# A last feed-forward whose units run as 512-column products over a high and a low operand, with one eviction for two tiles

## The chip, the cores and the metric

The kernel runs on one core of one Trainium2 chip. Its time is the device time of one launch, in microseconds. Three runs of the kernel before gave 2199.34, 2200.89 and 2201.28 us, so the median is 2200.89 us.

## The reference, cut to what matters

The program is two stacks of transformer blocks on 256 latent tokens of 1024 features. The second stack has two layers and carries 256 context tokens too. The change touches only the feed-forward of the very last layer, which works on the 256 latent tokens alone:

```python
# second_block, last layer (i = 1), latent tokens only
x = _layer_norm(alpha * x + g1 * y, ln1_g[i], ln1_b[i])
x = _layer_norm(alpha * x + g2 * _mlp(x * (1 + sc2) + sh2, mlp_w1[i], mlp_w2[i]), ln2_g[i], ln2_b[i])
# _mlp(a, w1, w2): hidden = relu(a @ w1) ** 2, 4096 wide; out = hidden @ w2
```

Products are in float32 quality. A number is held as a high part (rounded to the type that TensorE takes, `fp32r`) and a low part (the rest), and a product is high*high + high*low + low*high.

## The kernel before, in words

**Units.** Weights come in units of 128 x 2048 float32 (16 tiles of 128 x 128, 1 MB), by two DMA transfers of half a unit each, into a ring of three slots (`SLOTS = 3`). The transfer of unit u+3 is issued on the SP queue when TensorE has finished unit u. ScalarE rounds each half to `w_hi` (L1467), VectorE computes `w_lo = w_raw - w_hi` (L2156). Both do so two units ahead (`ahead(u)` splits unit u+2 in the turn of unit u). TensorE waits for `lo_split` of a half before it first uses that half.

**The last feed-forward** (`run_mlp(1)`) has 32 units: 4 up, 4 down, 4 up, 4 down, and so on, four quarters of each. I number them 0 to 31: up units are 0 to 3, 8 to 11, 16 to 19, 24 to 27; down units are 4 to 7, 12 to 15, 20 to 23, 28 to 31. An up quarter makes 8 tiles of the hidden layer (two per unit), and the down quarter behind it uses these 8 tiles in each of its four units. Units 0 to 3 (`plain_up`) work on an input that is normalized afterwards and are not part of the change, nor are the down units 4 to 7 and 28 to 31.

**A unit on TensorE** (`fm_unit`, `fm_tile`): two products, one after the other, each over 8 tiles k. For each k there are three matmuls of 256 columns into one PSUM bank: `w_hi` with the high operand, `w_hi` with the low operand, `w_lo` with the high operand. So a unit has 48 matmuls. A product goes to a bank of ring A (banks 0, 1) or ring D (banks 2, 3), and waits until the product two before in its ring is evicted. In unit 8, the first with freshly normalized operands, the two products are interleaved k by k, and each k waits for `operand`. In the first unit of a down quarter (12, 20, 28) tile k waits for `hid_ready`.

**Evictions of an up unit**, one tile at a time: ScalarE takes max(x, 0) from PSUM (L1491), VectorE squares (L3146), rounds to the high part (L3148), and computes the low part (L2156 with `hid_both`), which raises `hid_ready`. Behind the second tile come the two `w_lo` halves of unit u+2. **Of a down unit**: VectorE adds each tile to the sum `y_acc` (in `qk`, L3222), then splits, and in units 12 to 15 and 20 to 23 computes one tile of the modulation of another layer part (`ada_tile`, L2191, two passes of 128 x 1024). ScalarE has no eviction there and casts weights as they land. In units 16 to 19 VectorE also rescales two tiles of X (L2260), in 24 to 27 it adds two tiles of the sum to X (L3243).

**Fresh operands.** During down units 4 to 7 VectorE normalizes two tiles of X per unit, ScalarE modulates them (L2064) and rounds (L1498), VectorE makes the low part (L2156 with `a_both`). The last two tiles, 6 and 7, are made behind the `w_lo` halves of the turn of unit 7.

**The four wide stages** of the first stack (`run_ffn`) already use 512-column matmuls: `wide_high` multiplies `w_hi` with the high and low operand side by side into a whole bank of 512 columns, `wide_lows` adds `w_lo` times the high operand into the second half of the bank, and the eviction adds the two halves (ScalarE copy L1892, VectorE add L2936). Their up part takes the same 16 wide and 16 narrow matmuls per unit as the changed units do.

The order of the work is written out by hand; there is no scheduler.

Of the kernel before, what the change touches and what calls it, by code (L numbers as in the profile page):

```python
# [117 lines left out]

def last_ring(quarter, j):
    return "AD"[j % 2] if quarter < 3 else None  # L120
FIRST_SMALL = slice(0, SMALL["ones"].stop)
# [26 lines left out]
def program(nc, weights, small, x_t, c_rows, ctx_t, na_bias, na_bv, out_t):  # L148
    with ExitStack() as ctx:
# [147 lines left out]


        def pair_banks(j):
            return [(0, 1), (2, 3)][j % 2]  # L300
# [169 lines left out]
        plain_hi, plain_lo = (h[:, 6 * S:6 * S + KD * PLAIN].rearrange("p (k t) -> p k t", k=KD) for h in (hid_hi, hid_lo))  # L470
        last_hi, last_lo = ([h[:, c:c + S] for c in [S * k for k in range(6)] + [20 * S, 21 * S]] for h in (hid_hi, hid_lo))
        mean_row = p_ring[:, 2, LAT]
        plain_out = [p_ring[:, j, LAT] for j in range(2)]
# [59 lines left out]
        def _(pe):  # L533
# [823 lines left out]
            def run_mlp(i):  # L1357
# [6 lines left out]
                def hidden(c):  # L1364
                    return [(hi[k][:, c], lo[k][:, c]) for k in range(KD)]

                def plain_up():
                    plain = [(plain_hi[:, k, :], plain_lo[:, k, :]) for k in range(KD)]

                    def arrives(k):  # L1370
                        pe.wait_ge(plain_ready, k + 1)
                        if k == 5:
                            n["ln"] += 1
                            n["chain"] += 1
                            layer_totals(slice(0, S), TOK, KD)
                            layer_mean(slice(0, S), MEAN)

                    def spreads(k):
                        if k == 2:
                            layer_spread(0, S // P, SPREAD, 0)  # L1380

                    fm_unit(PLAIN_RINGS[0], plain, arrives, True)
                    fm_unit(PLAIN_RINGS[1], plain, spreads, True)
                    for rings in PLAIN_RINGS[2:]:
                        fm_unit(rings, plain)

                def up(many=4, quarter=3):
                    for j in range(many):
                        fm_unit(2 * (last_ring(quarter, j) or "A"), a)

                def down(q, many=4, between=None):
                    for j in range(many):
                        early = i == 1 and q == 0 and j == 0
                        fm_unit(2 * (last_ring(q if i == 1 else 3, j) or "D"), hidden(slice(0, T)),
                                None if j else lambda k: wait(pe, hid_ready, hid0 + KD * q + k + 1), early, between if j == 1 else None)

# [5 lines left out]
                for q in range(3):  # L1402
                    down(q)
                    if i == 1 and q == 0:
                        operands()
                    up(quarter=q + 1 if i == 1 else 3)
                down(3, 4 if i else 2, lambda: shift_mean(T))
# [46 lines left out]
        def _(act):  # L1454
# [572 lines left out]
            def run_mlp(i):  # L2027
# [15 lines left out]
                def plain_up(j):  # L2043
                    u, _ = next_unit(PLAIN_RINGS[j])
                    ahead(u)
                    for m in range(2):
# [10 lines left out]
                        nc.scalar.copy(last_hi[k], y).then_inc(hid_h, 1)  # L2057

                def modulated(k):
                    n["norm"] += 1  # L2060
# [6 lines left out]
                for q in range(4):  # L2067
                    for j in range(4):
                        if i == 0 and q == 0:
                            up("DAEA"[j], j > 0)  # L2070
                        elif q == 0:
                            plain_up(j)
                        else:
                            up(last_ring(q if i == 1 else 3, j) or "A")
                    if i == 1 and q == 0:
                        for j in range(5):
                            for k in (2 * j - 2, 2 * j - 1) if j else []:
                                modulated(k)
                            if j < 4:
                                skip(2 * last_ring(q, j))  # L2080
                    elif q < 3:
                        for j in range(4):
                            skip(2 * (last_ring(q if i == 1 else 3, j) or "D"))
                if i == 0:
                    stream_layer()
                else:
                    layer_units(cols, T, i)

# [53 lines left out]
        def _(dve):  # L2142
# [986 lines left out]
            def run_mlp(i):  # L3129
# [8 lines left out]
                def up(q, ring="A", split_ahead=True):  # L3138
# [55 lines left out]
                for at in range(3):  # L3194
                    for q in range(4):
                        if i == 0 and at == 0:
                            up(q, "DAEA"[q], q > 0)
                        elif at == 0:
                            plain_up(q)
                        else:  # L3200
                            up(q, last_ring(at if i == 1 else 3, q) or "A")
                        if i == 1 and at == 2:
# [4 lines left out]
                    for q in range(4):  # L3207
                        ring = last_ring(at if i == 1 else 3, q) or "D"
                        u, made = next_unit(2 * ring)
# [24 lines left out]
                if i == 1:  # L3234
                    dve.wait_ge(ada_sum, 2 * MOD_TILES + 4)
                    finish_mods(MOD_LAST, MOD_TILES)
                    sync()
                for q in range(4):
                    up(q)
                    for k in (2 * q, 2 * q + 1):  # L3240
# [12 lines left out]
                else:  # L3253
                    layer_units((1, 5), cols, T)

# [219 lines left out]
```

## Time and profile before

| | |
|---|---|
| median of 3 runs | 2200.89 us |
| the profiled execution | 2199.01 us |
| its span in the trace | 2197.2 us |
| TensorE matmul busy | 2170.6 us, 99% |
| VectorE busy | 1782.4 us, 81% |
| ScalarE busy | 1171.2 us, 53% |
| mean granted TensorE clock | 0.998 of 2.4 GHz |

The profiled execution took 1.81 us more than its span, which is what lies around the traced part. "Busy" of TensorE is a union of modelled intervals that overlap, so 99% says that it never waits for long, not that each matmul runs at its shortest. The work behind the last matmul (the final normalization and the store of the output) takes the rest of the span.

### The profile page before, as it was taken

To read this page: it belongs to the slowest core of one execution; us is meant where nothing else is said; L and a number is where in the kernel's file an instruction comes from. 1 tells how busy PE (TensorE), PEld (TensorE's weight loads), DVE (VectorE), ACT (ScalarE), POOL (GpSimd) and SP (SyncE) were. 2 spreads that over 40 slices of the span, in tenths; PEclk is the share of its full clock that TensorE was granted. 3 is DMA by queue.
4 is the path that set the end of the run, shared out by engine and by line. 5 is a ranking of instruction groups with operands and counts; after the bars stand their busy time and mean duration, and the time that the engine had idled before them with its cause. 6 is when DMAs were issued, how large, how long until landed. Compare 5 with 4: busy or idle time off the path is not lost.

```text
span 2197.2 us, 38028 instructions
## 1 busy us (share of the span) xinstructions
PE 2170.6 (99%) x15136; PEld 1946.0 (89%) x15136; DVE 1782.4 (81%) x3522; ACT 1171.2 (53%) x2051; POOL 0.2 (0%) x4
## 2 busy tenths in 40 slices
PE   9999999999999999999999999999999999999998
PEld 8888889898899988996988987898888889979998
DVE  8879978689887898888898777578877876478898
ACT  5776556565554655558655646452222236376533
POOL 0000000000000000000000000000000000000000
PEclk9999999999999999999999999999999999999999
DMA  8326665467665676770676531015454523435663
GB/s 274 121 90 234 220 211 198 161 214 235 195 219 175 208 241 201 220 221 22 228 238 201 176 125 58 20 62 179 158 186 167 167 79 106 135 98 167 208 237 119
DMA packets 115377, 372.04 MB, mean 169 GB/s; under 512 B 12416, under 2 KB 22272, under 8 KB 115200
## 3 DMA queue, kind: packets, MB, share of 16 engines
q1 hardware_dynamic: 106688, 359.97, 50.0%
q10 hardware_dynamic: 8512, 9.63, 1.4%
q8 instruction: 120, 1.97, 0.4%
q14 instruction: 57, 0.47, 0.1%
HBM read 367.46 MB, written 1.05 MB: 168 GB/s over the span
## 4 chain that ended last, share of the span: by engine, by line
PE 92%; DVE 6%; ACT 2%; issue 1%; ACTq 0%; DVEq 0%
PE ps L538 88%; DVE hid_f L2551 1%; PE ps L882 1%; DVE hid_f L2573 1%; PE ps L818 1%; PE ps L866 1%; DVE w_lo L2156 1%; PE ps L988 0%; ACT p_ring L1607 0%; DVE X L2288 0%; PE ps L806 0%; DVE a_both L2156 0%; DVE X L2435 0%; DVE recip L2567 0%; ACT hid_f L1674 0%
## 5 line engine op out<-in xcount | busy, mean ns | idle before, releaser
L538 PE MATMUL ps<-a_both,w_hi 128*128 128x256 f32 (+1 forms) x4816 | 1028.4, 328 | 1.3 <-DVE a_both L2156 0.7
L538 PEld LDWEIGHTS ps<-a_both,w_hi 128*128 128x128 f32 x4816 | 806.3, 190 | 77.8 <-DVE a_both L2156 3.3
L2156 DVE TENSOR_TENSOR w_lo<-w_raw,w_hi 128x1024 fp32r<-128x1024 f32 (+3 forms) x630 | 703.9, 1144 | 75.1 <-ACT w_hi L1467 59.4
L538 PE MATMUL ps<-a_both,w_lo 128*128 128x256 f32 (+1 forms) x3112 | 693.7, 292 | 0.0
L1467 ACT CAST w_hi<-w_raw 128x1024 fp32r<-128x1024 f32 (+3 forms) x428 | 404.0, 973 | 272.6 <-DMA w_raw<-weights 270.9
L538 PEld LDWEIGHTS ps<-a_both,w_lo 128*128 128x128 f32 x3112 | 506.4, 191 | 17.2
L538 PE MATMUL ps<-hid_both,w_hi 128*128 128x512 f32 (+2 forms) x2184 | 512.9, 347 | 1.0 <-DVE hid_both L2348 0.5
L538 PEld LDWEIGHTS ps<-hid_both,w_hi 128*128 128x128 f32 x2184 | 377.5, 189 | 54.5 <-issue 5.4
L538 PE MATMUL ps<-hid_both,w_lo 128*128 128x256 f32 (+2 forms) x1444 | 330.0, 304 | 0.0
L538 PEld LDWEIGHTS ps<-hid_both,w_lo 128*128 128x128 f32 x1444 | 229.9, 191 | 14.0
L1475 ACT CAST w_hi<-w_raw 128x1024 fp32r<-128x1024 f32 (+1 forms) x198 | 202.3, 1022 | 0.2 <-DMA w_raw<-weights 0.2
L1892 ACT COPY p_ring<-ps 128x512 f32<-128x512 f32 x88 | 51.7, 587 | 135.5 <-PE ps L538 117.7
L2191 DVE CUSTOM_DVE_ANT_1 ps<-pe_sb,X 128x1024 f32<-128x1024 f32 x96 | 118.0, 1229 | 1.6
L1491 ACT ACTIVATE p_ring<-ps 128x512 f32<-128x512 f32 (+1 forms) x56 | 28.2, 506 | 169.1 <-PE ps L538 168.8
L2191 DVE CUSTOM_DVE_ANT_0 ps<-pe_sb,c_late 128x1024 f32<-128x1024 f32 x88 | 108.2, 1230 | 3.2
L1674 ACT ACTIVATE hid_f<-hid_f,negmax 128x128 f32<-128x128 f32 (+1 forms) x192 | 94.1, 498 | 14.1 <-DVE negmax L2551 13.6
L538 PE MATMUL ps<-w_hi,a_both 128*128 128x256 f32 (+1 forms) x448 | 93.3, 304 | 0.0
L2936 DVE TENSOR_TENSOR p_ring<-ps,p_ring 128x512 f32<-128x512 f32 x88 | 60.6, 688 | 38.6 <-ACT p_ring L1892 38.6
L538 PEld LDWEIGHTS ps<-w_hi,a_both 128*128 128x128 f32 x448 | 72.1, 191 | 4.2 <-issue 1.4
L2156 DVE TENSOR_TENSOR hid_both<-t_ring,hid_both 128x256 fp32r<-128x256 f32 (+1 forms) x152 | 72.2, 477 | 3.2 <-ACT hid_both L2057 1.3
L1895 ACT ACTIVATE p_ring<-p_ring 128x256 f32<-128x256 f32 x88 | 36.8, 419 | 58.6 <-DVE p_ring L2938 58.6
L538 PE MATMUL ps<-w_lo,a_both 128*128 128x256 f32 (+1 forms) x224 | 67.4, 301 | 0.0
(261 smaller groups left out, 1934.2 us busy)
## 6 DMA issues: line engine op xcount, KB each, us to landing
w_raw<-weights SPq DMA_DIRECT2D x496, 512.0 KB, 4.5
pe_sb<-weights SPq DMA_DIRECT2D x96, 512.0 KB, 5.4
w_raw<-weights SPq DMA_DIRECT2D x64, 384.0 KB, 3.3
w_raw<-weights SPq DMA_DIRECT2D x64, 320.0 KB, 3.7
pe_sb<-na_bias ACTq DMA_DIRECT2D x32, 128.0 KB, 2.2
X<-x_t SPq DMA_DIRECT2D x2, 512.0 KB, 6.7
X<-c_rows ACTq DMA_DIRECT2D x2, 512.0 KB, 7.6
qk<-qk ACTq DMA_DIRECT2D x4, 256.0 KB, 6.4
```

The lines of the kernel that those rows point to most:

```text
L538: return nc.tensor.matmul(out, stationary, moving, start=start, stop=stop)
L818: last = nc.tensor.matmul(ps[:, o, q], v, t_ring[:, e, t], start=j == 0, stop=j == len(it["pv"]) - 1, skip_group_check=True)
L866: last = nc.tensor.transpose(ps[:, banks[r], at // 2:at // 2 + HD], p_pair(name, b)[half(r), at:at + P], ident[half(r), half(r)])
L1467: nc.scalar.copy(high, whole).then_inc(hi_split, 1)
L1475: nc.scalar.copy(w_hi[:, u % SLOTS, c], raw(u, c)).then_inc(hi_split, 1)
L1491: nc.scalar.activation(dst, src, func or ACT.Copy, **kw).then_inc(taken[ring], 1)
L1674: last = nc.scalar.activation(at, at, ACT.Exp, bias=negmax[:, i % 4, x:x + 1], scale=-1.0, accum_out=sums[:, i % 4, x:x + 1])
L1892: nc.scalar.copy(low_slot, ps[:, at, S:2 * S]).then_inc(low_copied, 1)
L1895: nc.scalar.activation(gate_sum, gate_sum, ACT.Silu).then_inc(silu_done, 1)
L2156: return v.tensor_tensor(out, a, b.bitcast(F32), ALU.subtract)
L2191: v.tensor_tensor_reduce(to, ada_w[:, a % 2, :].rearrange("p (a b) -> p a b", b=S), c, 1.0, 0.0, ALU.mult, ALU.add, mod[:, a, s_:s_ + 1]). ...
L2936: v.tensor_tensor(both, ps[:, made[0][0]:made[1][0] + 1, 0:S], low_slot, ALU.add).then_inc(taken["A"], 1)
```

## The change

The 12 up units 8 to 11, 16 to 19 and 24 to 27 and the 8 down units 12 to 15 and 20 to 23 are issued by a new function `wide_unit`: the 512-column products of both tiles first, then the 256-column `w_lo` products of both. It waits at its start until both banks of its ring are free. ScalarE copies the second halves of both banks in one instruction (`low_halves`), VectorE adds them to the first halves in one instruction of 512 columns (`both_halves`), and all that follows is 512 columns wide for the two tiles of a unit together: the squared relu in one instruction on VectorE, the high part on ScalarE, the low part on VectorE. One `w_lo` half of unit u+2 now stands between the square and the low part, on VectorE and likewise on ScalarE. All these units alternate between ring A and ring D (before, quarter 3 did not), and unit 28 moves to ring A.

On TensorE:

```diff
+                def wide_unit(ring, xs, arrives=None):
+                    u, made = start_unit(2 * ring)
+                    for _, p, _ in made:
+                        start_product(ring, p)
+                    lower = bank_pair(made).start
+                    for at, (bank, _, _) in enumerate(made):
+                        for k, x in enumerate(xs):
+                            if arrives and at == 0:
+                                arrives(k)
+                            wide_high(ps[:, bank, :], u % SLOTS, (bank - lower) * KD + k, x, k == 0, False)
+                    for bank, _, (ready, _) in made:
+                        wide_lows(ps[:, bank, :], u % SLOTS, (bank - lower) * KD, xs, True).then_inc(ready, 1)
...
-                def up(many=4, quarter=3):
+                def up(many=4):
                     for j in range(many):
-                        fm_unit(2 * (last_ring(quarter, j) or "A"), a)
+                        if i == 1:
+                            wide_unit(last_ring(j), wide_parts(LAT), operand_at)
+                        else:
+                            fm_unit("AA", a)
...
+                        if i == 1 and q in (1, 2):
+                            wide_unit(last_ring(j), last_both, None if j else arrives)
+                            continue
+                        ring = last_ring(j) if i == 1 and q == 0 else "A" if i == 1 and j == 0 else "D"
+                        fm_unit(2 * ring, hidden(slice(0, T)), None if j else arrives, early, between if j == 1 else None)
```

On ScalarE:

```diff
+                def low_halves(ring):
+                    u, made = next_unit(2 * ring)
+                    for _, _, (s_, count) in made:
+                        wait(act, s_, count)
+                    if lows:
+                        before, p = lows[-1]
+                        act.wait_ge(taken[before], p + 1)
+                    lows.append((ring, made[1][1]))
+                    nc.scalar.copy(low_slot, ps[:, bank_pair(made), S:2 * S]).then_inc(low_copied, 1)
+                    return u
+                def wide_up(j):
+                    u = low_halves(last_ring(j))
+                    split_half(u + 2, 0)
+                    r = cnt.next("relu")
+                    cnt.next("relu")
+                    act.wait_ge(hid_f, r + 2)
+                    nc.scalar.copy(last_pairs[j][0], t_ring[:, j % 2, :]).then_inc(hid_h, 2)
+                    split_half(u + 2, 1)
...
+                    elif i == 1 and q < 3:
+                        for j in range(4):
+                            ahead(low_halves(last_ring(j)))
```

On VectorE:

```diff
+                def both_halves(made, ring, j):
+                    both = gate_up_slot[j % 2]
+                    for m in made:
+                        ready(m)
+                    n["low_part"] += 1
+                    dve.wait_ge(low_copied, n["low_part"])
+                    v.tensor_tensor(both, ps[:, bank_pair(made), 0:S], low_slot, ALU.add).then_inc(taken[ring], 2)
+                    dve.wait_ge(taken[ring], made[1][1] + 1)
+                    return both
+                def wide_up(j):
+                    ring = last_ring(j)
+                    u, made = next_unit(2 * ring)
+                    both, y = both_halves(made, ring, j), t_ring[:, j % 2, :].rearrange("p (a t) -> p a t", a=2)
+                    r, h = cnt.next("relu"), cnt.next("hid")
+                    cnt.next("relu")
+                    cnt.next("hid")
+                    dve.wait_ge(hid_ready, h)
+                    v.scalar_tensor_tensor(y, both, 0.0, both, ALU.max, ALU.mult).then_inc(hid_f, 2)
+                    split_half(u + 2, 0)
+                    dve.wait_ge(hid_h, h + 2)
+                    minus(last_pairs[j][1], t_ring[:, j % 2, :], last_pairs[j][0]).then_inc(hid_ready, 2)
+                    split_half(u + 2, 1)
+                    ada_tiles()
+                def wide_down(j):
+                    ring = last_ring(j)
+                    u, made = next_unit(2 * ring)
+                    both, y = both_halves(made, ring, j), y_acc[:, 2 * j:2 * j + 2, 0:S]
+                    step(v.tensor_tensor(y, y, both, ALU.add))
+                    ahead(u)
+                    ada_tiles()
```

TensorE, the start of down unit 12, before (`hid_both` holds the hidden tiles; `taken_A` says that ring A is evicted):

```order
L538 MATMUL ps<-hid_both,w_hi 128x256 [waits hid_ready,taken_A,lo_split]
L538 MATMUL ps<-hid_both,w_hi 128x256
L538 MATMUL ps<-hid_both,w_lo 128x256
L538 MATMUL ps<-hid_both,w_hi 128x256 [waits hid_ready]
L538 MATMUL ps<-hid_both,w_hi 128x256
L538 MATMUL ps<-hid_both,w_lo 128x256
```

The same place and the unit behind it (13, ring D) after the change:

```order
L546 MATMUL ps<-hid_both,w_hi 128x512 [waits taken_A,hid_ready,lo_split]
L546 MATMUL ps<-hid_both,w_hi 128x512 [waits hid_ready] x7
L546 MATMUL ps<-hid_both,w_hi 128x512 [waits lo_split]
L546 MATMUL ps<-hid_both,w_hi 128x512 x7
L546 MATMUL ps<-hid_both,w_lo 128x256 x16
L546 MATMUL ps<-hid_both,w_hi 128x512 [waits taken_D,lo_split]
L546 MATMUL ps<-hid_both,w_hi 128x512 x15
L546 MATMUL ps<-hid_both,w_lo 128x256 x16
```

The eight tiles are now reached one matmul apart, where they were three apart. A unit on ring A waits for the second half of its weights before its ninth matmul. A unit on ring D has no such wait later on, because its first product falls on the upper bank (the count of products in ring D is odd there) and so uses the second half first: it waits for both halves at its start.

VectorE, the turn of up unit 11, before (`t_ring` is the square, `hid_both` the hidden tile):

```order
L3146 TENSOR_TENSOR t_ring<-p_ring 128x256 [waits taken_D,hid_ready]
L3148 CAST hid_both<-t_ring 128x256 [waits hid_f]
L2156 TENSOR_TENSOR hid_both<-t_ring,hid_both 128x256 [waits hid_h]
L3146 TENSOR_TENSOR t_ring<-p_ring 128x256 [waits taken_D]
L3148 CAST hid_both<-t_ring 128x256 [waits hid_f]
L2156 TENSOR_TENSOR hid_both<-t_ring,hid_both 128x256 [waits hid_h]
L2156 TENSOR_TENSOR w_lo<-w_raw,w_hi 128x1024 [waits hi_split] x2
```

and after, with the turn of down unit 12 behind it up to its `w_lo` halves:

```order
L3222 TENSOR_TENSOR p_ring<-ps,p_ring 128x512 [waits unit_done,low_copied,mid_ready]
L3234 SCALAR_TENSOR_TENSOR t_ring<-p_ring 128x512 [waits hid_ready,taken_D]
L2215 TENSOR_TENSOR w_lo<-w_raw,w_hi 128x1024 [waits hi_split]
L2215 TENSOR_TENSOR hid_both<-t_ring,hid_both 128x512 [waits hid_h]
L2215 TENSOR_TENSOR w_lo<-w_raw,w_hi 128x1024 [waits hi_split]
L3222 TENSOR_TENSOR p_ring<-ps,p_ring 128x512 [waits unit_done,low_copied,mid_ready]
L3245 TENSOR_TENSOR qk<-qk,p_ring 128x2x256 [waits taken_A]
L2215 TENSOR_TENSOR w_lo<-w_raw,w_hi 128x1024 [waits hi_split] x2
```

The low part of the two hidden tiles now stands behind one `w_lo` half, and the eviction begins only when the whole unit is done.

## Rows read from the trace of the kernel before

**Rows 1.** The page, section 1: busy time, share of the span, instructions.
```profile
PE 2170.6 (99%) x15136; PEld 1946.0 (89%) x15136; DVE 1782.4 (81%) x3522; ACT 1171.2 (53%) x2051; POOL 0.2 (0%) x4
```
**Rows 2.** Busy time by stretch, last feed-forward: stretch, length, busy of each engine, clock, DMA.
```profile
2100.00:2150.00 50.00, 50.00 (x419) 50.00 (x418) 45.98 (x79) 19.90 (x26) 0.00 (x0) 1.00 0.67 230
```
**Rows 3.** Chain that ended last, in order of time: start, us, what.
```profile
2001.89 183.06 PE ps L538 x1522
```
**Rows 4.** TensorE in order of time at unit 8: start us, us, instruction.
```profile
2046.12 0.40 PE L538 MATMUL ps<-a_both,w_hi 128*128 128x256 f32 x2
2046.48 0.40 PE L538 MATMUL ps<-a_both,w_hi 128*128 128x256 f32 x2
```
**Rows 5.** The same view in a wide stage: sixteen 512-column products.
```profile
619.68 3.79 PE L538 MATMUL ps<-hid_both,w_hi 128*128 128x512 f32 x16
```
**Rows 6.** ScalarE in order of time, wide stage, copies three units apart.
```profile
222.85 0.59 ACT L1892 COPY p_ring<-ps 128x512 f32<-128x512 f32 x1 [1.89 <-PE ps L538]
...
239.55 0.59 ACT L1892 COPY p_ring<-ps 128x512 f32<-128x512 f32 x1 [0.94 <-PE ps L538]
```
**Rows 7.** ScalarE, evictions of units 10 and 11 of the last feed-forward.
```profile
2063.66 0.38 ACT L1491 ACTIVATE p_ring<-ps 128x256 f32<-128x256 f32 x1 [2.50 <-PE ps L538]
...
2069.42 0.38 ACT L1491 ACTIVATE p_ring<-ps 128x256 f32<-128x256 f32 x1 [2.50 <-PE ps L538]
```
**Rows 8.** VectorE in order of time, the last hidden tile of unit 11.
```profile
2069.84 0.42 DVE L3146 TENSOR_TENSOR t_ring<-p_ring 128x256 f32<-128x256 f32 x1 [1.16 <-ACT p_ring L1491]
...
2070.62 0.42 DVE L2156 TENSOR_TENSOR hid_both<-t_ring,hid_both 128x256 fp32r<-128x256 f32 x1
```
**Rows 9.** VectorE, the turn of unit 7: weights, then operand tiles 6 and 7.
```profile
2047.39 2.35 DVE L2156 TENSOR_TENSOR w_lo<-w_raw,w_hi 128x1024 fp32r<-128x1024 f32 x2
2049.65 0.75 DVE L2156 TENSOR_TENSOR a_both<-p_ring,a_both 128x256 fp32r<-128x256 f32 x2
```
**Rows 10.** VectorE in a wide stage: the add that follows a copy of rows 6's kind.
```profile
240.17 0.69 DVE L2936 TENSOR_TENSOR p_ring<-ps,p_ring 128x512 f32<-128x512 f32 x1 [0.48 <-ACT p_ring L1892]
```
**Rows 11.** Groups of instructions by form: busy us, mean ns of one, idle before.
```profile
L2156 DVE TENSOR_TENSOR hid_both<-t_ring,hid_both 128x512 fp32r<-128x512 f32 x32 | 22.2, 693 | 1.1
L3148 DVE CAST hid_both<-t_ring 128x512 fp32r<-128x512 f32 x32 | 13.7, 427 | 1.1
L2156 DVE TENSOR_TENSOR w_lo<-w_raw,w_hi 128x1024 fp32r<-128x1024 f32 x494 | 590.2, 1219 | 64.3 <-ACT w_hi L1467 49.1 <-ACT w_hi L1475 15.0
L1467 ACT CAST w_hi<-w_raw 128x1024 fp32r<-128x1024 f32 x312 | 318.5, 1047 | 245.8 <-DMA w_raw<-weights 244.3 <-issue 0.8
L1997 ACT CAST a_both<-qk 128x512 fp32r<-128x512 f32 x8 | 5.0, 621 | 14.7 <-DVE qk L3077 14.7
```
**Rows 12.** VectorE, the turn of down unit 13 and the start of the next.
```profile
2081.22 2.35 DVE L2156 TENSOR_TENSOR w_lo<-w_raw,w_hi 128x1024 fp32r<-128x1024 f32 x2
2083.49 1.22 DVE L2191 CUSTOM_DVE_ANT_0 ps<-pe_sb,c_late 128x1024 f32<-128x1024 f32 x1
...
2085.96 0.42 DVE L3222 TENSOR_TENSOR qk<-ps,qk 128x256 f32<-128x256 f32 x1
2086.64 0.42 DVE L3222 TENSOR_TENSOR qk<-ps,qk 128x256 f32<-128x256 f32 x1 [0.27 <-PE ps L538]
```
**Rows 13.** VectorE, the X work in units 16 and 24.
```profile
2102.03 0.73 DVE L2260 TENSOR_SCALAR X<-X,alpha_g,alpha_b 128x256 f32<-128x256 f32 x2
...
2148.56 0.88 DVE L3243 SCALAR_TENSOR_TENSOR X<-qk,mod,X 128x256 f32<-128x256 f32 x2
```
**Rows 14.** SP queue and ScalarE: a unit's weights from issue to cast.
```profile
2075.11 0.81 SPq L514 DMA_DIRECT2D w_raw<-weights  x2
...
2080.27 1.05 ACT L1467 CAST w_hi<-w_raw 128x1024 fp32r<-128x1024 f32 x1 [0.21 <-DMA w_raw<-weights]
```
**Rows 15.** TensorE by stretch at the program's end: length, busy (x), clock, DMA.
```profile
2184.00:2186.00 2.00, 0.96 (x9) 1.00 0.00 0
...
2190.00:2192.00 2.00, 0.00 (x0) 0.50 0.02 4
```

More of the change, by code:

```diff
@@ L116, with last_ring @@
 PLAIN_RINGS = ["AA", "DD", "AA", "DD"]
-def last_ring(quarter, j):
-    return "AD"[j % 2] if quarter < 3 else None
+def last_ring(j):
+    return "AD"[j % 2]
 FIRST_SMALL = slice(0, SMALL["ones"].stop)
@@ L296, in unit, with bank_pair @@
             return u, made
+        def bank_pair(made):
+            lower = min(bank for bank, _, _ in made)
+            return slice(lower, lower + 2)
         def pair_banks(j):
@@ L471, in program @@
         last_hi, last_lo = ([h[:, c:c + S] for c in [S * k for k in range(6)] + [20 * S, 21 * S]] for h in (hid_hi, hid_lo))
+        last_both = [(hi, lo, hid_both[:, :, S * k:S * k + S])
+                     for hi, lo, k in zip(last_hi, last_lo, [*range(6), 20, 21])]
+        last_pairs = [[h[:, S * k:S * k + 2 * S] for h in (hid_hi, hid_lo)] for k in (0, 2, 4, 20)]
         mean_row = p_ring[:, 2, LAT]
@@ L1385, in plain_up, with arrives @@
                         fm_unit(rings, plain)
-                def up(many=4, quarter=3):
+                def up(many=4):
                     for j in range(many):
-                        fm_unit(2 * (last_ring(quarter, j) or "A"), a)
+                        if i == 1:
+                            wide_unit(last_ring(j), wide_parts(LAT), operand_at)
+                        else:
+                            fm_unit("AA", a)
                 def down(q, many=4, between=None):
+                    def arrives(k):
+                        wait(pe, hid_ready, hid0 + KD * q + k + 1)
                     for j in range(many):
                         early = i == 1 and q == 0 and j == 0
-                        fm_unit(2 * (last_ring(q if i == 1 else 3, j) or "D"), hidden(slice(0, T)),
-                                None if j else lambda k: wait(pe, hid_ready, hid0 + KD * q + k + 1), early, between if j == 1 else None)
+                        if i == 1 and q in (1, 2):
[3 more added lines that the diff above has]
+                        fm_unit(2 * ring, hidden(slice(0, T)), None if j else arrives, early, between if j == 1 else None)
                 if i == 0:
@@ L1405, in run_mlp @@
                         operands()
-                    up(quarter=q + 1 if i == 1 else 3)
+                    up()
                 down(3, 4 if i else 2, lambda: shift_mean(T))
@@ L2072, in run_mlp @@
                             plain_up(j)
+                        elif i == 1:
+                            wide_up(j)
                         else:
-                            up(last_ring(q if i == 1 else 3, j) or "A")
+                            up()
                     if i == 1 and q == 0:
@@ L2086, in run_mlp @@
                 else:
-                    layer_units(cols, T, i)
+                    layer_units(cols, T, i, first="A")
             def run_na(_):
@@ L3207, in run_mlp @@
                     for q in range(4):
-                        ring = last_ring(at if i == 1 else 3, q) or "D"
+                        if i == 1 and at > 0:
+                            wide_down(q)
+                            continue
+                        ring = last_ring(q) if i == 1 else "D"
                         u, made = next_unit(2 * ring)
@@ L3237, in run_mlp @@
                     sync()
+                sync()
                 for q in range(4):
-                    up(q)
+                    if i == 1:
+                        wide_up(q)
+                    else:
+                        up(q)
                     for k in (2 * q, 2 * q + 1):
@@ L3253, in run_mlp @@
                 else:
-                    layer_units((1, 5), cols, T)
+                    layer_units((1, 5), cols, T, first="A")
             def run_na(_):
```

10 lines of the change are left out of this document (6 added, 4 removed).

## The prediction

> **What bounds the kernel now.** I read the page's busy times first, then the table of stretches, then the chain, then the engines in order of time around the changed units. TensorE is busy for 99% of the span [rows 1], and for the whole of a stretch inside the last feed-forward at full clock, while VectorE is busy for 46 of its 50 us there [rows 2]. The chain of waits through this stage is one piece of matmuls, 183.06 us long [rows 3]. So two things count: how fast matmuls follow each other, and whether TensorE has to wait, which it does not do now. VectorE has some 8% to give, and that is a mean over quarters that differ.
>
> **What the wide form saves.** In unit 8 three matmuls of 256 columns start every 0.36 us (2046.12 and 2046.48 [rows 4]), 0.120 us each, so a unit is 48 x 0.120 = 5.76 us; the evictions of units 10 and 11 confirm it, 2069.42 - 2063.66 = 5.76 us [rows 7]. A 512-column matmul takes about 0.227 us: 16 of them stand in 3.79 us, of which the last one's tail, some 0.16 us, lies over the next [rows 5]. A pair of 256-column matmuls costs 0.240, so merging it saves 0.013 us, and 16 pairs save 0.21 us. The wide stage has units of just this mixture (16 wide, 16 narrow), and three of them take 239.55 - 222.85 = 16.70 us, 5.57 each [rows 6]. I take 5.57, as it is measured with all that goes with it: 0.19 us per unit, and **20 units save 3.8 us** (4.3 by the single matmuls, as the other end).
>
> The Trainium skill ("TensorE: Matmul & The Clock Gate", section "Back-to-back issue gap") gives N / 2.4 GHz plus about 2.5 ns between matmuls. This trace does not agree: 256 columns are 106.7 ns and take 120. By that rule the 320 merged pairs would save 320 x 2.5 ns = 0.8 us (an estimate from that page), and the total below would be 3 us later.
>
> **What the change lets become late.** The chunks of work behind a unit get fewer and longer, and they start later. I measure from E, the moment at which TensorE has issued the unit's last matmul; ScalarE starts the eviction 0.26 us later (the next unit of the row at 2069.42 starts at 2069.16 by the 5.76 grid from 2046.12 [rows 4, 7]).
>
> *Operands at unit 8.* VectorE makes operand tiles 6 and 7 behind the weights in the turn of unit 7, from 2049.65 on: two in 0.75 us, so done at 2050.07 and 2050.40 [rows 9]. Nothing in this part moves. Before, unit 8 went through both products k by k and came to tile 7 at 2046.12 + 7 x 0.72 = 2051.16, late enough. Now it comes to tile 7 after seven wide matmuls, at 2046.12 + 1.59 = 2047.71, and has to wait until 2050.40 plus some 0.05 us of signalling. **A wait of 2.75 us.** Queued behind it is the whole of TensorE's stream.
>
> *Hidden tiles at units 12, 20 and 28.* Before, the last hidden tile of unit 11 was ready at 2070.62 + 0.42 = 2071.04 [rows 8], 1.88 us after E = 2069.16, and wanted at 7 x 0.36 = 2.52 us: hidden. After the change both last tiles pass one chain: ScalarE's copy of 512 columns, start E + 0.26, 0.59 long [rows 6], to 0.85; VectorE's add, 0.04 later, 0.69 long [rows 10], to 1.58; the square of 512 columns, 0.03 later. The trace has no such form from SBUF; its nearest are 0.69 (a subtraction of two 512-column tiles) and 0.43 (a copy) [rows 11]. Having two tensor inputs it is nearer the first: 0.69, to 2.30. Then ScalarE rounds 512 columns, 0.62 [rows 11], to 2.96. VectorE meanwhile has begun a `w_lo` half at 2.22; two halves take 2.27 us [rows 12], so one holds it until 3.36; then the low part, 0.69, to 4.05, and 4.10 at TensorE. TensorE wants tile 6 after six wide matmuls, at 1.36. **A wait of 2.74 us at unit 12 and at unit 20.** Unit 28 keeps its three matmuls per tile and wants tile 6 at 6 x 0.36 = 2.16: **1.94 us.** Before, tile 6 had been evicted half a unit earlier. The ends: if the `w_lo` half did not stand between, 3.00 + 0.69 + 0.05 = 3.74, a wait of 2.4; if a late cast of weights on ScalarE (1.05 [rows 11]) pushed the rounding, up to 3.8.
>
> *VectorE in the down quarters.* Before, a down unit cost it two adds, two halves (2.27) and a modulation tile (2.47, from 2083.49 to 2085.96), and it then waited 0.27 us for the next tile [rows 12]. Now it has an add of 0.69 + 0.03, an add into the sum of 0.61 (512 columns without a wait behind it), 2.27 and 2.47: 6.07 us against 5.57 of TensorE. It falls back 0.50 us per unit, so it starts 1.5 us late on unit 15. Its second half for unit 17 is then ready at E + 4.58 + 1.5 + 0.05 = 6.13, and unit 17 is on ring D, wants both halves at its start at 5.57, and waits 0.56. In up units it has add 0.72, square 0.61, half 1.14, low part 0.61, half 1.14 = 4.2 us, plus 0.65 for X [rows 13] in quarter 2, and makes the second half ready at E + 5.19, only 0.38 before a ring D unit wants it. Being 0.75 late at unit 17, it lets unit 19 wait 0.43. In quarter 3 it starts 0.5 later still (it completes the modulation first) and X costs 0.8 [rows 13]: 0.56 at unit 25, and at unit 27, after 1.37 of lateness at unit 25, 1.05. **Together 2.6 us**; this is the least sure term, between nothing (if VectorE is 0.5 us quicker per unit than I count) and 5.
>
> *What costs nothing.* The weights' transfers: the second half is cast 5.2 us after the issue at a unit's end [rows 14], and the new order on ScalarE needs it 1.7 us after the next E, at 7.3. The banks: a ring is taken two units later and evicted 1.6 us after E. A wait may also cost a restart of TensorE, which no row shows; between nothing and 0.3 us for each of 8 waits (the first matmul then no longer lies over another). I take nothing.
>
> **The sum.** -3.8 + 2.75 + 2.74 + 2.74 + 1.94 + 2.6 = +8.9 us. The work behind the last matmul is the same. From the profiled execution, 2199.01, this gives 2207.9; the median of the runs is 1.9 us above it, so **2209.8 us**, 0.4% slower. A measurement of this kernel tells about 0.2% (4.4 us) from no change.
>
> **Rivals.**
> 1. *The late weights do not come about*, only the four waits for operands and hidden tiles: +6.3, **2207.2**. For it: VectorE's lateness rests on two instructions that the trace does not show in this form. Against it: the modulation tile alone takes 2.47 us. Chance 0.2.
> 2. *The wide form gains what it does in the wide stages and nothing waits*: -3.8, **2197.1**, not slower. Its place is the end of units 11, 19 and 27 and the operands of unit 8. It decides from the point at which the tiles are ready within 1.36 us (1.59) of the next unit's start, where I count 4.1 (4.3). For it: the same form runs in the wide stages with TensorE full. Against it: no stage there consumes a tile so soon after its eviction, and copy and two passes alone are 2 us. Chance 0.1, with all that ends within 0.2% or below.
> 3. *The clock falls in a wait.* At the end of the program TensorE is half idle from 2184 on and still has its full clock; it has the half level, 1.2 GHz, in the stretch from 2190 on, in which it does nothing [rows 15]. No wait in the body is as long as the 2.7 us above. Should the clock fall in each of the four and stay low for one unit of 5.57 us, these take twice as long: 4 x 5.57 = 22 us more, **2232**. Against it: 2.7 us of rest against 5 us of thin work and rest in the one case that the rows show. Chance 0.06.
>
> On 3 the Trainium skill (the same page, section "HAM oscillation — how this bites in real kernels") says that waits between bursts of matmuls bring the clock down again and again. By that rule the time would be the one of rival 3 if these waits are long enough; that the clock does fall without work, rows 15 agree.
>
> **How the numbers follow.** My forecast has 0.64, the rivals 0.2, 0.1 and 0.06. The lower ends of the waits (2.75 + 2 x 2.4 + 1.6 = 9.1) with the larger saving and no late weights give +4.9, 2205.8; the upper ends (restarts 2.4, late weights 5) give +13.7, 2214.6. I reach a little toward rival 2 below: **2203.5 to 2214.5**. Slower by over 0.2% means above 2205.3: 0.86. Within 0.2%: 0.10. Faster: 0.04.
>
> **What would show it.** In the changed trace TensorE should wait for `a_both` once, at unit 8, some 2.7 us; for `hid_both` three times, 2.7, 2.7 and 1.9; and a few times for `w_lo`, under 1.1 us each, at ring D units. Copies of ScalarE inside a quarter should be 5.57 us apart. The prediction is wrong if the units are closer together than that, if the waits on `hid_both` are under 2 us or absent, or if the clock column is below 1.00 in the stage.

## The result and the profile after

The changed kernel takes **2222.98 us** (median of 4 runs, 2215.9 to 2227.36), the kernel before 2201.09 in the same session (4 runs, 2199.34 to 2208.37): ratio 1.009, interval [1.0067, 1.0112]. It is slower, as forecast, but by 22 us and not by 9, and outside the range that I gave. The same kernel, run a second time later together with the kernel before, gave 2215.36 (7 runs, 2214.3 to 2218.45), ratio 1.0054 [1.0034, 1.0074]. I call such a group of runs a submission. That two submissions of one program differ by 7.6 us is half of the story.

First TensorE at unit 8 in the changed kernel, in order of time (start us, us, instruction, and in brackets the idle time before it and who ended it). It answers to [rows 4].

```profile
2061.65 1.55 PE L546 MATMUL ps<-a_both,w_hi 128*128 128x512 f32 x6
2065.68 2.68 PE L546 MATMUL ps<-a_both,w_hi 128*128 128x512 f32 x10 [2.49 <-DVE a_both L2215]
```

Two things stand here. There are six wide matmuls and then 2.49 us of idle time, the first wait of the forecast. And the unit begins at 2061.65, where it began at 2046.12 before [rows 4]: 15.5 us are already lost ahead of the first instruction that the change touches. The view of busy time by stretch (stretch, length, busy of TensorE, weight load, VectorE, ScalarE, POOL, granted clock, DMA share, GB/s) shows where, in the changed kernel:

```profile
75.00:80.00 5.00, 5.00 (x39) 4.31 (x39) 3.78 (x4) 3.19 (x5) 0.00 (x0) 0.82 0.50 167
80.00:85.00 5.00, 5.00 (x25) 5.00 (x25) 3.32 (x13) 4.86 (x7) 0.00 (x0) 0.50 0.45 184
...
995.00:1000.00 5.00, 5.00 (x26) 5.00 (x25) 0.00 (x0) 1.76 (x8) 0.00 (x0) 0.50 0.00 0
```

and the kernel before in a stretch of the same work, 45 matmuls at full clock where 25 stand above:

```profile
80.00:85.00 5.00, 5.00 (x45) 5.00 (x45) 3.91 (x17) 4.94 (x7) 0.00 (x0) 1.00 0.33 135
```

TensorE is full in both. Added up over windows of 1 us, its clock stands at the half level (1.2 GHz) for 13.7 us from 78 on and for 17.1 us from 989 on. Half of each is lost: 6.8 + 8.5 = 15.3 us.

The waits of the changed stage, grouped (who waits, for whom, then us in total, times, longest):

```profile
PE ps L546 <- DVE hid_both L2215: 7.3, 3, 2.7
PE ps L546 <- DVE w_lo L2215: 2.7, 4, 1.1
PE ps L546 <- DVE a_both L2215: 2.5, 1, 2.5
```

These are the ones that I named, in number and place, and in length to within 0.3 us. The clock behind the wait of unit 12, again TensorE in order of time and then by stretch:

```profile
2091.08 3.83 PE L546 MATMUL ps<-hid_both,w_hi 128*128 128x512 f32 x10 [2.68 <-DVE hid_both L2215]
2094.71 2.43 PE L546 MATMUL ps<-hid_both,w_lo 128*128 128x256 f32 x16
```

```profile
2090.00:2092.00 2.00, 0.92 (x4) 0.78 (x5) 2.00 (x3) 0.94 (x1) 0.00 (x0) 1.00 1.03 422
2092.00:2094.00 2.00, 2.00 (x7) 1.56 (x6) 0.20 (x1) 0.00 (x0) 0.00 (x0) 0.52 0.25 100
2094.00:2096.00 2.00, 2.00 (x11) 1.81 (x10) 0.00 (x0) 0.00 (x0) 0.00 (x0) 0.62 0.00 0
```

Ten wide matmuls stand in 3.83 us where ten behind unit 8's wait stand in 2.68. TensorE had waited 2.68 us and worked for about 1 us when the clock fell. From the start of unit 8 to the end the stage is 164.0 us long, 151.1 before: +12.9.

In the second submission's profile hardly anything is lost ahead (unit 8 starts at 2046.96; in the second profile of the kernel before it starts at 2046.77), but the clock falls behind all three waits for hidden tiles:

```profile
2078.00:2080.00 2.00, 2.00 (x6) 1.60 (x5) 0.00 (x0) 0.00 (x0) 0.00 (x0) 0.50 0.00 0
...
2130.00:2132.00 2.00, 2.00 (x12) 1.99 (x11) 0.00 (x0) 0.00 (x0) 0.00 (x0) 0.55 0.00 0
...
2180.00:2182.00 2.00, 2.00 (x11) 2.00 (x11) 0.50 (x2) 0.24 (x1) 0.00 (x0) 0.50 0.00 0
```

Each time 3.4 us at the half level, which cost 1.7. Its stage is 2213.6 - 2046.96 = 166.6 us.

### The profile page after: what moved, and what is told of

Its sections match the earlier page's. It is cut to its first block and busy times, and to the rows that moved or that the text cites. A ratio compares the mean times of both kernels' runs of the same rounds, so it can differ in the third digit from the quotient of the medians.

```text
span 2225.6 us, 37421 instructions
## 1 busy us (share of the span) xinstructions
PE 2187.0 (98%) x14816; PEld 1943.8 (87%) x14816; DVE 1785.9 (80%) x3486; ACT 1180.9 (53%) x2059; POOL 0.2 (0%) x4
## 5 line engine op out<-in xcount | busy, mean ns | idle before, releaser
L546 PE MATMUL ps<-a_both,w_hi 128*128 128x256 f32 (+1 forms) x4624 | 1005.6, 334 | 6.6 <-DVE a_both L2215 3.2
L546 PEld LDWEIGHTS ps<-a_both,w_hi 128*128 128x128 f32 x4624 | 781.1, 190 | 91.7 <-DVE a_both L2215 6.3
L546 PE MATMUL ps<-a_both,w_lo 128*128 128x256 f32 (+1 forms) x3112 | 664.0, 292 | 0.0
L546 PEld LDWEIGHTS ps<-a_both,w_lo 128*128 128x128 f32 x3112 | 493.9, 191 | 18.2
L1499 ACT CAST w_hi<-w_raw 128x1024 fp32r<-128x1024 f32 (+3 forms) x404 | 379.4, 970 | 244.7 <-DMA w_raw<-weights 243.2
L546 PE MATMUL ps<-hid_both,w_hi 128*128 128x512 f32 (+2 forms) x2056 | 499.4, 359 | 8.3 <-DVE hid_both L2215 7.3
L546 PEld LDWEIGHTS ps<-hid_both,w_hi 128*128 128x128 f32 x2056 | 361.5, 189 | 67.9 <-DVE hid_both L2215 9.1
L546 PE MATMUL ps<-hid_both,w_lo 128*128 128x256 f32 (+2 forms) x1444 | 310.7, 304 | 0.0
L1507 ACT CAST w_hi<-w_raw 128x1024 fp32r<-128x1024 f32 (+1 forms) x222 | 227.9, 1027 | 0.4 <-DMA w_raw<-weights 0.4
L1523 ACT ACTIVATE p_ring<-ps 128x512 f32<-128x512 f32 x32 | 19.0, 598 | 128.3 <-PE ps L546 128.0
```

Of the source, the lines that this page charges most:

```text
L546: return nc.tensor.matmul(out, stationary, moving, start=start, stop=stop)
L1499: nc.scalar.copy(high, whole).then_inc(hi_split, 1)
L1507: nc.scalar.copy(w_hi[:, u % SLOTS, c], raw(u, c)).then_inc(hi_split, 1)
L1523: nc.scalar.activation(dst, src, func or ACT.Copy, **kw).then_inc(taken[ring], 1)
```

## The experiments

Two theories for the part that the forecast missed. **A**: the clock falls because TensorE rests (in the three waits for hidden tiles), and the early falls are chance, which hits the kernel before as well. **B**: the change itself makes the clock fall, by its wide matmuls or by what it moves. The rows of clock below tell them apart. "Stage" is always from unit 8's first matmul to the end of the span.

**The kernel before, again.** No edit.

> The kernel before, unchanged. The changed kernel lost 15.5 us ahead of its changed part, in two stretches of identical code in which the granted clock was 0.50 (13 and 17 us long). Theory: such falls of the clock come at random in the two NSA stages, whatever the kernel; then of five more runs of this unchanged one some should show a mean clock below 0.997 and take 4 to 15 us more than 2200, and the profile's stage from unit 8 on (2046.1 to the end, 151.1 us) is as before. Rival: the change brings the falls about; then all runs lie within 2199 to 2202 with a mean clock of 0.998.

Measured: 2200.8 us (12 runs), ratio 0.9988 [0.997, 1.0006]. Nine runs at a mean clock of 0.998 take 2199.2 to 2201.2, three at 0.994 take 2208.0 to 2208.7. Beside the three submissions of experiments the kernel before ran 71 more times: 45 runs between 2199.2 and 2202.7, 23 between 2207.1 and 2208.7, 3 between 2213.9 and 2215.1. One stretch of 13.7 us at the half level costs 6.8, one of 17.1 costs 8.5: from the median of the lowest group, 2200.2, that gives 2207.0 to 2208.7, and two stretches give 2213.8 or more. The mean clocks of the three groups are 0.997 to 0.998, 0.994 to 0.995 and 0.991 to 0.992. So by time and mean clock an unchanged kernel has a long fall in 26 of 71 runs; where it lies no profile shows, as both profiles of the kernel before are of runs without one. Counted by time in the same way, with the first runs and these twelve, it is 30 of 87 for the kernel before and 30 of 90 for the changed kernel and its variants. That only the change brings it is refuted.

**The changed kernel, again.** No edit.

> The changed kernel, unchanged. Theory (random falls in identical code, waits in the changed part): a clean run takes 2210 us, others up to 15 us more, with the mean clock falling by 0.001 for every 4.4 us at half clock; from unit 8 on the profile shows about 163 us again. Rival (the change itself brings the early falls): every run is above 2214 with a mean clock of 0.996 or less.

Measured: 2215.36 us (7 runs), as told above: all seven at clocks of 0.995 to 0.997, none with an early fall. In the first submission three of four runs stood at 2221 to 2227 and clocks of 0.990 to 0.993, the fourth at 2215.9. So the median of the result carries about 7 us of chance, and 2215.4 is the changed kernel itself.

**Tiles 6 and 7 last** (`late`). Units 8, 12 and 20 take tiles 0 to 5 of both products and both operands first; unit 28 goes through its two products tile by tile (that is what `early` does).

```
+if arrives and (arrives is not operand_at or n["fresh"] is not None):
+    for part in (range(6), range(6, KD)):
+        for k in part:
+            arrives(k)
+            for bank, _, _ in made:
+                ...
+                mm(ps[:, bank, :], w_hi[...], xs[k][2], k == 0, False)
+        for bank, _, (ready, _) in made:
+            ...
+            last = wide_lows(ps[:, bank, :], ...)
+            ...
...
-early = i == 1 and q == 0 and j == 0
+early = i == 1 and q in (0, 3) and j == 0
```

> The changed kernel, but in units 8, 12 and 20 both products go through tiles 0 to 5 (wide and narrow) before either touches tiles 6 and 7, and unit 28 interleaves its two products. Tile 6 is then wanted 4.16 us after the unit's start (4.32 in unit 28) in place of 1.36 (2.16). Theory of the waits: the four waits of 2.5, 2.7, 2.7 and 1.9 us go, as does the fall of the clock behind the one at unit 12 (1.6 us): from unit 8 on 11 us less than the changed kernel, a clean run near 2199. Rival (the stage is slow through VectorE's load, and its time comes back as waits for weights): less than 5 us are won and the waits for w_lo grow to more than 6 us.

Measured: 2201.71 us (12 runs), ratio 0.9996 [0.9979, 1.0014]; the seven runs at 0.997 or 0.998 take 2199.4 to 2201.9, with a median of 2200.0. Its waits:

```profile
PE ps L546 <- DVE w_lo L2229: 2.6, 4, 1.1
```

All four operand waits are gone, and so is every fall of the clock in the stage, though its wide matmuls are as many as in the changed kernel. It is 15 us below the changed kernel's own 2215.4, where I had expected 11, with 9.7 us of idle time taken away: more went than the waits. B, in the form that the wide matmuls lower the clock, does not survive this.

**And the lower bank's product first** (`both`). As `late`, and wide units begin with the product whose `w_lo` half is ready first.

```
-for at, (bank, _, _) in enumerate(made):
+for at, (bank, _, _) in enumerate(sorted(made, key=lambda m: m[0])):
```

> As late, and in each wide unit the product of the lower bank comes first, so that units on ring D want the second half of their weights only 1.8 us after their start. Theory: the waits for w_lo (2.7 us in four places) go too, and what is left is the saving of the wide form: from unit 8 on about 147.5 us, 3.6 us less than the kernel before (151.1), a clean run at 2197. Rival (VectorE becomes the bound once nothing else waits): waits for w_lo of 2 us or more remain and the stage takes 150 us or more.

Measured: 2200.07 us (12 runs), ratio 0.999 [0.9972, 1.0008]; the eight runs at clock 0.998 have a median of 2199.1, the kernel before's runs at 0.998 or 0.997 in the same submission one of 2200.2. Its stage is 149.5 us, 2.0 more than I expected and just under the rival's 150: three waits for `w_lo` are left, 1.1 us in all, so a part of the rival is true. This is the best version, 1.1 us under the kernel before, and by its interval not to be told from it.

**The rests filled with work** (`fill`). This is the decisive experiment. The tiles come no earlier; TensorE repeats the unit's first matmul until they do, 10 or 11 times in the wide units and 15 times (`fill`) at unit 28.

```
+if arrives:
+    arrives(0)
+    for _ in range(10 if arrives is operand_at else 11):
+        if arrives is not operand_at or n["fresh"] is not None:
+            wide_high(ps[:, made[0][0], :], ..., xs[0], True, True)
...
+for _ in range(fill if j == 0 else 0):
+    tile_at(0)
+    mm(ps[:, bank, 0:T], w_hi[:, u % SLOTS, 0:P], xs[0][0], True, True)
```

> The changed kernel with idle time turned into work. TensorE repeats the first matmul of the unit, into the bank that the unit then starts anew, before it comes to the tiles it has to wait for: 10 times at unit 8, 11 times at units 12 and 20 (512 columns, 0.227 us each: 2.3 and 2.5 us), 15 times at unit 28 (256 columns, 0.120 each: 1.8 us). What it waits for is ready at the same time as before, so the path is as long and only the rest shrinks to 0.1 to 0.2 us. Theory A (the clock falls because TensorE rests; each of the three falls of some 3.4 us at the half level costs 1.7 us): clock 1.00 all through the stage, stage from the start of unit 8 to the end 166.6 - 5.1 = 161.5 us, undisturbed runs near 2209.5 to 2210. Theory B (the falls belong to the wide matmuls or to the load of this stage, and would come without the rests): falls in the stage as in the changed kernel, stage 166 to 167, 2214 to 2215. If both, A and a filler that costs something itself: 2211.

Measured: 2211.24 us (9 runs), ratio 1.0045 [1.0028, 1.0062]; seven runs at clock 0.998 take 2210.4 to 2211.7. The wait of unit 12, and the stretch around it:

```profile
2076.15 2.56 PE L546 MATMUL ps<-hid_both,w_hi 128*128 128x512 f32 x10 [0.19 <-DVE hid_both L2224]
```

```profile
2046.00:2100.00 54.00, 53.64 (x299) 46.31 (x298) 40.63 (x56) 25.33 (x33) 0.00 (x0) 1.00 0.61 202
2100.00:2150.00 50.00, 48.89 (x275) 42.38 (x274) 44.72 (x63) 22.37 (x28) 0.00 (x0) 1.00 0.65 220
2150.00:2196.00 46.00, 44.22 (x320) 41.59 (x319) 39.83 (x65) 19.14 (x28) 0.00 (x0) 1.00 0.36 120
```

The wide matmuls resume at the same moment as before (2076.15, in the changed kernel 2076.34), the rest is 0.19 us, and the clock stays at its full level throughout. The kernel does more work and is 4.8 us quicker (2215.4 against 2210.6, the median of these seven). Theory A is shown for the falls in the stage: take the rests away, by order as in `late` or by work as here, and these falls go. I had expected 2209.5 to 2210 and a stage of 161.5; the lowest runs take 2210.4, the stage 161.8. The two runs at 2219.0 and 2219.5, clock 0.994, have a long fall like those of the kernel before.

**Half of each rest filled** (`half`): 5, 6, 6 and 7 repeats in place of 10, 11, 11 and 15.

> As fill, with about half of each rest turned into work: 5, 6, 6 and 7 repeated matmuls, so rests of 1.3 us at units 8, 12 and 20 and 1.1 at unit 28. The path is again as long. If any rest of about a microsecond makes the clock fall: 2214 to 2215, with three or four falls in the stage. If the length of the rest decides, and only those of 1.9 us and more did it: no fall, 2209.5 to 2210.

Measured: 2212.45 us (9 runs), ratio 1.0056 [1.0036, 1.0075]; its lowest four take 2209.9 to 2211.2. In its profile the four rests are 1.29, 1.32, 1.32 and 1.07 us and the clock is 1.00 behind each:

```profile
2127.11 2.58 PE L546 MATMUL ps<-hid_both,w_hi 128*128 128x512 f32 x10 [1.32 <-DVE hid_both L2224]
```

```profile
2130.00:2134.00 4.00, 4.00 (x26) 3.55 (x25) 1.56 (x3) 2.31 (x3) 0.00 (x0) 1.00 0.33 86
```

Rests of 1.1 to 1.3 us are harmless there; two runs in the middle (2212.5 and 2212.9, clock 0.997) had a fall or two somewhere. The profile has one, at 2004, ahead of the stage.

**Only the down units narrow again** (`narrow_down`).

```
-if i == 1 and q in (1, 2):
+if i == 1 and q > 3:
...
-    ahead(low_halves(last_ring(j)))
+    skip(2 * last_ring(j))
...
-if i == 1 and at > 0:
+if i == 1 and at > 3:
```

> One part of the change alone: the 12 up units stay wide with both tiles evicted together, the 8 down units of quarters 1 and 2 are 256-column products again, each tile evicted by itself. By the terms of the forecast: the wide form gains 12 x 0.19 = 2.3; unit 8 waits 2.5; units 12, 20 and 28 all want hidden tile 6 at 2.16 us and get it at 4.10, so each waits 1.94 (5.8 in all); VectorE has its old work in the down units and falls back less, so 0 to 0.5 of late weights. Sum +6.0 to +6.5 against before, 2207 for undisturbed runs if no clock falls; with a fall of 1.7 us behind each of the three waits of 1.9 us, 2212. If the wide down units and not the up units were what costs, it would stand at 2202.

Measured: 2211.06 us (12 runs), ratio 1.0049 [1.0031, 1.0068]; three runs at clock 0.998 take 2208.2 to 2208.5. Its waits:

```profile
PE ps L546 <- DVE hid_both L2215: 6.0, 3, 2.2
PE ps L546 <- DVE a_both L2215: 2.5, 1, 2.5
```

So the joint eviction of the up units is what costs, and the waits for `w_lo` (none here) belong to the wide down units' load on VectorE, as forecast. 2207 was over 1 us too low for those three runs. In the profile, of a run at 0.997, the clock fell behind two of the three waits (2078 and 2173), between my two cases.

**Only the bank order** (`banks`): the one-line edit of `both`, by itself.

> The changed kernel with one edit: a wide unit computes the product of the lower bank first, whose low part of the weights is the half that is ready first. Units on ring D then need the second half of w_lo 5.6/2 us later. By the forecast's term the four waits for w_lo (0.6, 0.35, 0.6 and 1.1, together 2.6 us) go and nothing else moves: 2.6 us less than the changed kernel, undisturbed 2212 to 2212.8, waits for operands and hidden tiles as in the changed kernel. Rival: VectorE stays as late as it is, and what TensorE doesn't wait for there it waits for at units 20 and 28, whose hidden tiles come out of the same backlog: no gain, 2214 to 2215, with longer waits for hid_both.

Measured: 2217.8 us (6 runs), ratio 1.0067 [1.0046, 1.0088]; three runs carry an early fall, the other three take 2213.6 to 2214.6. Its waits:

```profile
PE ps L546 <- DVE hid_both L2215: 7.7, 3, 2.7
PE ps L546 <- DVE w_lo L2215: 0.6, 1, 0.6
```

Three of the four waits for `w_lo` are gone and the stage is 164.1 us, 2.5 less than the changed kernel's 166.6. The undisturbed runs lie 0.8 us or more above the 2212 to 2212.8 that I expected, and a little of the rival is true too: VectorE is as late as it was, and the wait at unit 28 grows from 1.92 to 2.34.

**The two halves of the repair** (`only8`, `only_hid`): `late` with unit 8 as in the changed kernel, and `late` with unit 8 alone mended.

```
-if arrives and (arrives is not operand_at or n["fresh"] is not None):
+if arrives and arrives is not operand_at:                        # only8
+if arrives is operand_at and n["fresh"] is not None:             # only_hid
```

> The changed kernel with the waits for hidden tiles taken away (units 12 and 20 consume tiles 6 and 7 of both operands last, unit 28 goes through both products tile by tile), the wait for operand tiles at unit 8 left. By the terms: as late, which stood 0.2 us below the kernel before, plus the wait of 2.4 us: undisturbed runs at 2202 to 2203. In four profiles the clock did not fall behind unit 8's wait, though it is as long as the others; if that is no accident, clock 1.00 in the stage here too and 2202.5; if it is chance, some runs show one fall of 3.4 us more and stand 1.7 higher, 2204.2.

Measured: 2204.2 us (12 runs), ratio 1.0017 [1.0, 1.0033]; the five lowest runs take 2202.6 to 2203.5, as expected, three more 2204.1 to 2205.6. The wait is there and nothing happens behind it:

```profile
2059.50 2.66 PE L546 MATMUL ps<-a_both,w_hi 128*128 128x512 f32 x10 [2.46 <-DVE a_both L2229]
```

> The other half: unit 8 consumes tiles 6 and 7 of both operands last and does not wait, the waits for hidden tiles at units 12, 20 and 28 stay (2.7, 2.7, 1.9). By the terms: the changed kernel's 2215.3 less 2.4, 2212.9 with three falls of 1.7 us, 2211.2 with two, 2207.8 with none. If the first wait had been what sets off the falls behind the later ones, there would be none and 2208.

Measured: 2212.64 us (7 runs), ratio 1.0051 [1.0032, 1.0071], six of them 2212.0 to 2214.8, with the clock down for 3.4 us behind each of the three waits (from 2076, 2127 and 2178). That is my case of three falls, 2212.9; the first wait does not set off the later falls.

## Why the prediction was wrong

The direction, the waits and their causes were right; the time was not. Taken by its own steps:

**The wide form's saving** was right. Copies of ScalarE inside a quarter, in the second profile of the changed kernel:

```profile
2099.17 0.59 ACT L2102 COPY p_ring<-ps 128x512 f32<-128x512 f32 x1 [3.09 <-PE ps L546]
2104.74 0.59 ACT L2102 COPY p_ring<-ps 128x512 f32<-128x512 f32 x1 [3.08 <-PE ps L546]
2111.13 0.59 ACT L2102 COPY p_ring<-ps 128x512 f32<-128x512 f32 x1 [0.52 <-issue]
```

5.57 us apart, as taken from the wide stage [rows 6]. `both`, which has hardly any waits, is 1.5 us shorter in the stage than before with 1.1 us of idle time left, so it gained at least 2.6, and 3.8 is nearer than the 0.8 that the other rule I weighed would give.

**The four waits** were right in their working (2.4 to 2.5, 2.68, 2.68 and 1.92 us of idle time; forecast 2.75, 2.74, 2.74 and 1.94). The chain behind unit 11 in the same profile, ScalarE's cast and VectorE around it:

```profile
2073.08 0.69 DVE L3222 TENSOR_TENSOR p_ring<-ps,p_ring 128x512 f32<-128x512 f32 x1 [1.22 <-ACT p_ring L2102]
2073.86 0.69 DVE L3234 SCALAR_TENSOR_TENSOR t_ring<-p_ring 128x512 f32<-128x512 f32 x1
2074.47 1.22 DVE L2215 TENSOR_TENSOR w_lo<-w_raw,w_hi 128x1024 fp32r<-128x1024 f32 x1
2075.60 0.69 DVE L2215 TENSOR_TENSOR hid_both<-t_ring,hid_both 128x512 fp32r<-128x512 f32 x1
```

```profile
2074.64 0.62 ACT L2111 CAST hid_both<-t_ring 128x512 fp32r<-128x512 f32 x1 [0.75 <-DVE t_ring L3234]
```

The square of 512 columns takes 0.69, of the two rows that I chose between [rows 11] the right one, and the low part stands behind one `w_lo` half.

**The restart, taken at nothing, is a term.** I gave it 0 to 0.3 us for each wait and took the lower end. The copies show it: from 2104.74 to 2111.13 is 6.39, or 0.82 more than a unit, where the wait shows 0.59 of idle time. In the rows a matmul that follows another starts some 0.2 us before that one's end [rows 4, 5], and behind a wait that is lost. In `fill`, whose clock is clean, unit 8 takes 2.83 more than a unit, units 12 and 20 2.97 and 2.99, the `w_lo` waits 0.83, 0.57, 0.85 and 1.34 (3.6 together, 2.6 forecast). With 2.1 at unit 28 (it starts at 2173.85 in the changed kernel, wants tile 6 at 2176.01 and resumes at 2178.10), -3.8 + 2.8 + 6.0 + 2.1 + 3.6 = **+10.7** in place of +8.9 (the forecast's terms as written add up to +9.0), and `fill`'s stage is 161.8 us against 151.1, which is 10.7.

**The step that failed is the clock.** The forecast's sum has no term for it, and rival 3, the fall behind waits, had a chance of 0.06, because the only rest with a fall that the trace showed was longer. It called the event unlikely and large, 5.57 us for each of four waits. The sign of being wrong that it named, a clock below 1.00 in the stage, is what the traces show. The fall is likely and small: in five profiles with those waits the clock fell behind 12 of 15 waits for hidden tiles, for 3.4 us each time, so 1.7 us a fall and up to 5.1 a run. 2200.2 + 10.7 + 5.1 = 2216.0 with all three, and the runs without an early fall lie at 2214.3 to 2218.45. With the early falls left out, the changed kernel is 2215.4, 5.6 above the forecast: 1.8 of restarts and 5.1 of clock, less 0.7 because the undisturbed kernel before stands at 2200.2 and not at 2200.9; 0.6 of that sum is not found again. Even so it lies outside the range, whose upper end had room for restarts and late weights and none for the clock.

**And the measurement's spread was taken too narrow.** I had three runs of the kernel before, all within 2 us, and concluded that 4.4 us can be told. It has a second place 7 to 8 us higher in a third of its runs. The median of four runs of the changed kernel fell into it.

On the Trainium skill's section on clock oscillation ("TensorE: Matmul & The Clock Gate", "HAM oscillation — how this bites in real kernels"), which I cited for rival 3: the runs agree that waits between pieces of matmuls bring the clock down again and again. The waits in the Trainium skill's case are of some 3 to 5 us; here rests of 1.9 to 2.7 us were enough, and those of 1.1 to 1.3 in `half` were not. The Trainium skill also has the clock stay up where the work between waits is long against them. The early falls do not fit that: they come with no wait, TensorE being busy for 5.00 of 5 us.

What stays open. Why unit 8's wait, 2.4 to 2.5 us long, has no fall behind it in any of five profiles (the changed kernel twice, `narrow_down`, `banks`, `only8`), where waits of 1.9 elsewhere have one. Why three of the 15 waits for hidden tiles have none: units 20 and 28 in the first profile of the changed kernel, unit 20 in `narrow_down`. And what starts the early falls; the profiles give only their place (below).

## What to carry to other kernels

Evicting two tiles together saves instructions but makes the last one late, so before it is done where the next unit consumes those tiles, compare the eviction's whole chain with the moment at which they are wanted; ordering the consumer so that the late tiles come last took back all 15 us here. Price a wait of TensorE as its idle time plus 0.2 to 0.4 us for the restart, plus 1.7 us for the clock behind waits like those of 1.9 and 2.7 us here, and if it can't be removed, fill it: repeating a matmul whose result is overwritten was worth 4.8 us. And look at the granted clock of every run before two medians are compared.

## What was not expected of the hardware

- The clock's falls come in fixed lengths. Added up over windows of 1 us, every stretch at the half level inside the program was 3.4, 13.7 or 17.1 us long, which is one, four and five times 3.4, in all twelve profiles; the program's end apart.
- The long ones come without a wait of TensorE, at the same place of the program: from about 983 in `late`, `banks` and `only8`, from 989 in the changed kernel (which was 6.8 us late by then), and once from 78, at the same step of the earlier layer. There 256-column products are followed by thin ones: 64 columns, then eight with only 64 rows of operand. TensorE in order of time in `late`:

```profile
982.92 0.28 PE L546 MATMUL ps<-w_lo,hid_both 128*128 128x64 f32 x1
983.13 1.35 PE L546 MATMUL ps<-qk 64*128 64x128 f32 x8
```

  "Busy" doesn't say that these products fill the engine as wide ones do: three of 64 columns take 0.34 us here, nearly as long as three of 256 columns, 0.36. The other profiles pass this place at full clock. A difference of code there was not tried, so that the thin products start the falls is not shown.
- A 3.4 us fall also came at about 2004 (2010 where an early fall had delayed it) in five of the ten profiles of changed kernels, behind two rests of 0.5 and 0.4 us close together; none in the two of the kernel before. The same two rests stand in `fill` and in the second profile of the kernel before without a fall, so they are at most a part of the cause.
